# The last four slabs of each stage by token row, and the pieces behind them in column halves, in a two-block kernel

## The chip, the cores and the metric

One core of a Trainium2 chip runs the whole program. The metric is device microseconds of that core, the median of three runs. Lower is better.

## The reference, cut to what matters

Two transformer blocks in float32, one behind the other, on 256 tokens of width 2048. Each block is a mixer and a feed-forward part, and both have the same frame:

```python
h = rms_norm(x, g_pre_ffn) * (1.0 + scale_f) + shift_f      # second block: rmsnorm(h, g)
f = (silu(h @ w_ffn_gate) * (h @ w_ffn_up)) @ w_ffn_down
x = x + gate_f * rms_norm(f, g_post_ffn)                    # second block: h + rmsnorm(f, g)
```

So every stage ends in a row sum over 2048 columns (the post norm), an addition into x, and a second row sum (the next pre norm), before the next matrix can begin. The second block puts 16 meta tokens ahead of the 256 (272 columns), and its feed-forward part has a causal convolution over three tokens behind the gate product.

## The kernel before, in words

**Precision.** Each float32 matrix product is made of three passes in fp32r: high part by high part, high by low, low by high. A weight unit of 128x2048 floats (1 MB) lands in one of the four buffers of `raw` (RING = 4). ScalarE copies each half (1024 columns) to `whi` (`split_hi`, L446), VectorE writes the rest to `wlo` (`split_lo`, L453). Both have four slots (SLOTS = 4), and a slot is free when TensorE has counted `used` for what was in it. `raw_done` counts finished splits; SyncE's loads and TensorE both wait on it.

**Two kinds of product.** In a `chunk` (L557) the weight is the stationary side and x transposed (`xh`, `xl`) the moving one: eight halves of 24 matmuls. In a `slab` (L579) the staged activations (`stg`, cast by GpSimd in `stage_tile`, L618) are stationary and the weight moves: per half and per token row (t = 0 or 1, 128 tokens each) six matmuls into two PSUM banks (`products`, L568), so 24 for a slab. Row 0 has banks 0 to 3, row 1 banks 4 to 7.

**A feed-forward part** (`pe_ffn`, L1060) has two groups of 6 and 5 chunk pairs (gate, up), each followed by its 24 or 20 slabs of w_down. The first slab of a group does row 0, and waits for `h_done` ahead of row 1, since banks 4 to 7 hold the up product until VectorE has taken it (L1691). In the second group of the first block the sum `gateF` is taken out of banks 0 to 3 (`gate_out`) ahead of all slabs. The last two slabs (`last_slabs`, L602) do row 0 of both, count `rows_done`, then row 1 of both. VectorE adds a group's banks into `accf` (`parts`, L1712).

**Between stages.** For a row: VectorE multiplies by the gain (`dve_gained`, L1651), ScalarE sums the squares of 2048 columns (L648), VectorE adds into x (`dve_post`, L1658), ScalarE sums the squares of x, VectorE scales the row (`dve_normed_row`, L673), TensorE turns it 128 columns at a time (L690), ScalarE takes each turned tile to `xf` (L739), and VectorE splits `xf` in groups of four tiles (`dve_split_x`, L748 and L749); a chunk waits once per two halves for such a group. Eight tiles are turned ahead of the chunk, four more behind its second half and four behind its fourth (`pe_turn_more`). `pe_idle` (L698) issues small matmuls in the pause. Stage 2 (into the second block) also normalizes and turns the 16 meta rows, `xms`, behind row 1's. GpSimd fetches them when all slabs are staged (L2054) and multiplies `gateF` by the gain `gpost2` (L2058).

The four stage ends: A, out-projection of block one (sum 4, then norm 1); B, end of the first feed-forward part (sum 5, then norm 2); C, out-projection of block two (sum 6, then norm 3); D, the end of the program (sum 7, then the store of x).

## Time and profile before

| | |
|---|---|
| median of three runs | 2427.38 us (2423.9 to 2430.56) |
| profiled execution, its own time | 2429.2 us |
| its span | 2427.4 us |
| TensorE busy with matmuls | 2313.0 us (95%) |
| VectorE, ScalarE, GpSimd busy | 1530.9, 1047.7, 127.9 us |
| DMA | 506.47 MB, mean 209 GB/s |

The chain that ended last is the shortest explanation of the span: each piece of it released the next. Busy time of another engine counts only where it stands in that chain.

### The profile page before, as it was taken

Reading aid. Unit: us, or ns where it says so; the run is one execution under the profiler, and the core shown is the slowest. Engines: PE = TensorE matmul, PEld = TensorE weight load, DVE = VectorE, ACT = ScalarE, POOL = GpSimd, SP = SyncE. Lnnn points to the kernel's source line nnn. Section 1 sums busy time; section 2 is a strip of 40 time slices with the busy share of each in tenths; the row PEclk is TensorE's granted clock in tenths of the full one; section 3 lists DMA queues with packets and bytes.
Section 4 is the critical chain, followed back from the end, with each engine's and each line's share of the span. In section 5 each row is a group of like instructions: output and inputs, shape, how many; then the busy total and the mean of one; then the engine's idle time right before and its main releaser. Section 6 shows DMA issues by size and latency. Waiting matters only on the chain.

```text
span 2427.4 us, 41656 instructions
## 1 busy us (share of the span) xinstructions
PE 2313.0 (95%) x16346; PEld 2159.0 (89%) x16346; DVE 1530.9 (63%) x1727; ACT 1047.7 (43%) x1227; POOL 127.9 (5%) x248
## 2 busy tenths in 40 slices
PE   3999989899999999999999999998999999999997
PEld 3899768899998899998799998798999978999986
DVE  7988689755544467654554898746566544556545
ACT  5463243534444334443443535645444433344343
POOL 0000014000001100001100000000000011000010
PEclk9999989999999999999999999899999999999999
DMA  9988849555555577864455553254555555555552
GB/s 397 421 333 312 347 159 383 187 190 190 182 184 189 194 257 283 283 202 166 158 161 178 165 174 121 71 174 140 191 182 181 190 176 192 188 189 174 191 189 104
DMA packets 162957, 506.47 MB, mean 209 GB/s; under 512 B 8096, under 2 KB 12496, under 8 KB 134048
## 3 DMA queue, kind: packets, MB, share of 16 engines
q1 hardware_dynamic: 161536, 500.28, 58.8%
q0 software_dynamic: 752, 3.48, 0.5%
q8 instruction: 63, 1.03, 0.2%
q10 hardware_dynamic: 576, 1.44, 0.2%
q14 instruction: 30, 0.25, 0.0%
HBM read 503.07 MB, written 2.10 MB: 208 GB/s over the span
## 4 chain that ended last, share of the span: by engine, by line
PE 87%; DVE 5%; DMA 5%; ACT 2%; issue 1%; SPq 0%; POOL 0%; ACTq 0%; DVEq 0%; POOLq 0%
PE pb L574 23%; PE pb L552 18%; PE pb L554 18%; PE pb L553 18%; DMA raw<-w_in 3%; PE pb L536 1%; PE pb L932 1%; PE pb L537 1%; PE pb L538 1%; DVE x L1658 1%; PE pb L690 1%; DMA raw<-w_ada 1%; DVE wlo L499 1%; DVE raw L464 0%; DVE wlo L453 0%
## 5 line engine op out<-in xcount | busy, mean ns | idle before, releaser
L453 DVE TENSOR_TENSOR wlo<-raw,whi 128x1024 fp32r<-128x1024 f32 (+1 forms) x712 | 863.7, 1222 | 746.2 <-ACT whi L446 744.6
L446 ACT ACTIVATE whi<-raw 128x1024 fp32r<-128x1024 f32 (+1 forms) x712 | 746.3, 1054 | 1083.7 <-PE pb L554 715.4
L552 PE MATMUL pb<-xh,whi 128*128 128x256 f32 (+2 forms) x3760 | 1063.0, 283 | 5.8 <-DVE xl L749 3.0
L553 PE MATMUL pb<-xl,whi 128*128 128x256 f32 (+2 forms) x3760 | 1062.5, 283 | 0.0
L554 PE MATMUL pb<-xh,wlo 128*128 128x256 f32 (+2 forms) x3760 | 1061.4, 282 | 0.0
L552 PEld LDWEIGHTS pb<-xh,whi 128*128 128x128 f32 x3760 | 710.0, 189 | 6.8 <-ACT xf L739 4.0
L553 PEld LDWEIGHTS pb<-xl,whi 128*128 128x128 f32 x3760 | 709.9, 189 | 0.0
L554 PEld LDWEIGHTS pb<-xh,wlo 128*128 128x128 f32 x3760 | 709.6, 189 | 0.0
L574 PE MATMUL pb<-whi,stg 128*128 128x512 f32 x1664 | 453.0, 393 | 15.5 <-DVE hb L1691 5.1
L574 PEld LDWEIGHTS pb<-whi,stg 128*128 128x128 f32 x1664 | 315.1, 190 | 85.5 <-issue 6.8
L574 PE MATMUL pb<-wlo,stg 128*128 128x512 f32 x832 | 258.5, 392 | 0.0
L574 PEld LDWEIGHTS pb<-wlo,stg 128*128 128x128 f32 x832 | 158.1, 190 | 33.2
L464 DVE CUSTOM_DVE_ANT_0 raw<-raw,gateF,bcol 128x2048 f32<-128x2048 f32 x47 | 112.0, 2393 | 11.9 <-DMA raw<-w_ada 8.1
L622 POOL CAST stg<-hTh 128x256 fp32r x88 | 35.4, 402 | 1443.4 <-PE pb L554 1052.0
L508 PE MATMUL pb<-xh,whi 128*128 128x256 f32 (+1 forms) x256 | 73.6, 288 | 14.8 <-DVE wlo L499 7.9
L2467 DVE SCALAR_TENSOR_TENSOR zT<-upad,colv,zT x180 | 75.7, 481 | 0.0
L536 PE MATMUL pb<-xh,whi 128*128 128x256 f32 x240 | 69.1, 288 | 4.3 <-DVE wlo L453 4.3
L509 PE MATMUL pb<-xl,whi 128*128 128x256 f32 (+1 forms) x256 | 72.9, 285 | 0.0
L510 PE MATMUL pb<-xh,wlo 128*128 128x256 f32 (+1 forms) x256 | 72.8, 284 | 0.0
L690 PE MATMUL pb<-kc,xs 128*128 128x128 f32 x128 | 25.3, 355 | 45.3 <-ACT xs L2195 31.8
L537 PE MATMUL pb<-xl,whi 128*128 128x256 f32 x240 | 68.5, 285 | 0.0
L538 PE MATMUL pb<-xh,wlo 128*128 128x256 f32 x240 | 68.3, 285 | 0.0
(372 smaller groups left out, 1601.1 us busy)
## 6 DMA issues: line engine op xcount, KB each, us to landing
raw<-w_ada SPq DMA_DIRECT2D x79, 1024.0 KB, 7.0
raw<-w_ffn_gate SPq DMA_DIRECT2D x44, 1024.0 KB, 5.2
raw<-w_ffn_up SPq DMA_DIRECT2D x44, 1024.0 KB, 5.2
raw<-w_ffn_down SPq DMA_DIRECT2D x44, 1024.0 KB, 4.8
raw<-w_gate SPq DMA_DIRECT2D x44, 1024.0 KB, 5.2
raw<-w_up SPq DMA_DIRECT2D x44, 1024.0 KB, 5.2
raw<-w_down SPq DMA_DIRECT2D x44, 1024.0 KB, 4.8
raw<-w_in SPq DMA_DIRECT2D x40, 1024.0 KB, 5.1
```

What stands on the lines that cost most here:

```text
L446: act.activation(to, src, ACT.Copy).then_inc(hi_ready, 1)
L453: dve.tensor_tensor(to, src, hi, ALU.subtract).then_inc(raw_done, 1)
L464: return dve.tensor_tensor_reduce(unit, unit, csb[:, :], g, b, ALU.mult, ALU.add, to)
L508: mm(o, whi[:, s, wt], xh[:, k, 0:SEQ], start=(k == 0 and n % 2 == 0), stop=False, skip_group_check=True)
L536: mm(o, whi[:, s, t], xh[:, k, 0:SEQ], start=(k == 0 and f % 2 == 0), stop=False, skip_group_check=True)
L537: mm(o, whi[:, s, t], xl[:, k, 0:SEQ], start=False, stop=False, skip_group_check=True)
L538: last = mm(o, wlo[:, s, t], xh[:, k, 0:SEQ], start=False, stop=(k == KT - 1), skip_group_check=True)
L552: mm(o, whi[:, s, t], xh[:, k, c0:c1], start=(k == 0), stop=False)
L553: mm(o, whi[:, s, t], xl[:, k, c0:c1], start=False, stop=False)
L554: last = mm(o, wlo[:, s, t], xh[:, k, c0:c1], start=False, stop=(k == KT - 1))
L574: last = mm(pb[:, 4 * t + 2 * hh + c, :], stg[:, s, part, t * P:(t + 1) * P], wt[:, ws, c * CW:(c + 1) * CW], start=first and part == 0 an ...
L2467: op = dve.scalar_tensor_tensor(acc, src, wt, acc, ALU.mult, ALU.add)
```

## The change

- `last_slabs_by_row`: at the end of each feed-forward part row 0 of the last four slabs is done first (two slabs before), then row 1's first column half of all four, then its second half; `rows_done` is counted after each of the first two. So that four slabs can be held, the last two go through further buffers (`whix`, `wlox`, `stgx`) over `xh`, `xl` and `tb`. At A the same is done with two slabs; C is not a slab stage.
- `first_slabs`: the first two slabs of a group do one row of both, then the other row of both. In the second group of block one row 1 comes first.
- Sums and norms of row 1 in column halves (`act_half_stats`, `dve_post_halves`, `dve_normed_row`, `parts` with one half, the store in three pieces). VectorE's order changes: `dve_post` of row 0 now stands behind row 1's first half (FFN: ahead of it), and at A behind both halves of row 1's gain.
- Turned tiles lie two to a bank (`turn_at`), x is split in pairs of tiles and a chunk waits once per half.
- The meta rows are scaled by ScalarE in place and turned in a bank of their own ahead of the rest (`pe_turn_meta`), and VectorE writes them to `xf`; `turn` no longer has meta instructions.

The core of the diff:

```diff
+    whix = nc.alloc_sbuf_tensor_at("whix", [P, SLOTS, HALF], F32R, offset=XH0)
...
+        at_least(act, used, w - SLOTS - skipped + 1 + i * nw)
...
+    def far_hi(u, w, h):
+        act.wait_ge(landed[u % RING], landed_at(u, 0, 0))
+        act.activation(whix[:, h, :], raw[:, u % RING, h % 2 * HALF:(h % 2 + 1) * HALF], ACT.Copy).then_inc(hi_ready, 1)
+    def far_lo(u, w, h):
+        dve.wait_ge(hi_ready, w + 1)
+        dve.tensor_tensor(wlox[:, h, :], raw[:, u % RING, h % 2 * HALF:(h % 2 + 1) * HALF], whix[:, h, :].bitcast(F32),
+                          ALU.subtract).then_inc(raw_done, 1)
...
+            if x_split is not None:
+                pe.wait_ge(sem("x_split"), x_split + h + 1)
...
+        ws = 2 * s + hh if far else (w + hh) % SLOTS
+        tile, hi, lo = (stgx, whix, wlox) if far else (stg, whi, wlo)
+        for part, wt in ((0, hi), (0, lo), (1, hi)):
...
+    def first_slabs(u, w, stg_n, order, freed):
+        for n, t in enumerate(order):
+            if t in freed:
+                pe.wait_ge(*freed[t])
+            for j in range(2):
+                if n == 0:
+                    pe.wait_ge(staged, stg_n + 2 * j)
+                for hh in range(2):
+                    if n == 0:
+                        pe.wait_ge(raw_done, 2 * (u + j) + hh + 1)
+                    last = products(w + 2 * j, j, t, hh, j == 0)
+                if n:
+                    last.then_inc(used, 2)
...
+    def last_slabs_by_row(u, w, stg_n, n, step):
+        def one(j, t, hh):
+            return products(w + 2 * j, j % 2, t, hh, far=j >= 2)
+        for j in range(n):
+            pe.wait_ge(staged, stg_n + 2 * j)
+            for hh in range(2):
+                pe.wait_ge(raw_done, 2 * (u + step * j) + hh + 1)
+                last = one(j, 0, hh)
+        last.then_inc(sem("rows_done"), 1)
+        for hh in range(2):
+            for j in range(n):
+                last = one(j, 1, hh)
+                if hh:
+                    last.then_inc(used, 2)
+            if hh == 0:
+                last.then_inc(sem("rows_done"), 1)
...
+    def act_half_stats(n, hh, src, ready):
+        act.wait_ge(*ready)
+        part, total = stat[:, n, PART_AT:PART_AT + 1], stat[:, n, 1:2]
+        act_link(act.activation(like(squares[:, 0:HALF], src), src, ACT.Square, accum_out=total if hh else part))
+        if hh:
+            act.activation(total, total, ACT.Sqrt, scale=1.0 / D, bias=part).then_inc(sem("rms"), 1)
+        else:
+            act_link(act.activation(part, part, ACT.Identity, scale=1.0 / D, bias=eps))
...
+    def act_x_stats(n, t, done):
+        if t == 0:
+            act_row_stats(n, [(0, x[:, 0, :])], lambda t: (sem(done), 1))
+            return
+        for hh in range(2):
+            act_half_stats(n, hh, x[:, 1, COLS[hh]], (sem(done), 2 + hh))
...
-        dve.tensor_scalar(to, src, rstd[0:r, n, t:t + 1], None, ALU.mult).then_inc(sem("normed"), 1)
-    def turn_bank(n, k):
+        for cs in COLS if t else (slice(0, D),):
+            dve.tensor_scalar(to[:, cs], src[:, cs], rstd[0:r, n, t:t + 1], None, ALU.mult).then_inc(sem("normed"), 1)
...
-        return [rows[1], rows[0], rows[2]] if n == 2 else rows
+            return k % 8, 0
+        return 4 + k // 2 % 4, k % 2 * SEQ
...
+        pe.wait_ge(sem("normed"), NORMED_AT[2])
+        for k in range(KT):
+            last = pt(pb[:, META_BANK, k * META:(k + 1) * META], xm0[:, k * P:(k + 1) * P], kc[0:META, K_ID:K_ID + META])
+        last.then_inc(sem("turned"), 1)
...
-            pe.wait_ge(sem("turned_out"), KT * n + 1)
-            pe_idle(6, 4)
-            pe.wait_ge(sem("turned_out"), KT * n + 8)
+            pe_idle(3, 0)
...
+        def more(k0, k1, ready):
             pe.wait_ge(sem("turned_out"), KT * n + ready)
-            rows = turn_rows_of(n)
-            for k in range(k0, k0 + 4):
+            pe.wait_ge(sem("normed"), NORMED_AT[n] + 3)
...
+        return {1: lambda: more(8, 12, 4), 3: lambda: more(12, 16, 8)}
...
-            act.wait_ge(sem("turned"), KT * n + k + 1)
+            if n and k >= 8 and k % 2 == 0:
+                between(k // 2)
+            act.wait_ge(sem("turned"), TURNED_AT[n] + (k | 1 if n else k) + 1)
...
-        for j, hs in enumerate(((0, 1), (2, 3), (4,), (5, 6, 7))):
-            first(hs)
-            dve.wait_ge(ready, before + 4 * j + 4)
-            ks = slice(4 * j, 4 * j + 4)
+        first((0,))
+        for h in range(8):
+            dve.wait_ge(ready, before + 2 * h + 2)
+            ks = slice(2 * h, 2 * h + 2)
             dve_link(dve.tensor_copy(xh[:, ks, lo:width], xf[:, ks, lo:width]))
             dve.tensor_tensor(xl[:, ks, lo:width], xf[:, ks, lo:width], xh[:, ks, lo:width].bitcast(F32),
                               ALU.subtract).then_inc(sem("x_split"), 1)
+            if h < 7:
+                first((h + 1,))
...
+            order, freed = (0, 1), {1: (sem("h_done"), c + n)}
...
+                order, freed[0] = (1, 0), (sem("gate_out"), 1)
...
+            first_slabs(u, w, st + 2, order, freed)
+            for j in (2, 3):
+                slab(u + j, w + 2 * j, st + 2 * (j + 1), j % 2, False)
...
+            if g:
+                last_slabs_by_row(u + m, w + 2 * m, st + 2 * (m + 1), 4, 1)
+            else:
...
+            if g:
+                for h in range(4):
+                    far_hi(u - 2 + h // 2, w - 4 + h, h)
...
+            act_half_stats(n, hh, accf[:, 1, COLS[hh]], (sem("part_done"), summed + hh + 1))
...
+        if not hh:
+            dve_row_scale(n, t, P)
+        cs = slice(0, D) if hh is None else COLS[hh]
         dve.wait_ge(*taken)
-        dve.scalar_tensor_tensor(res, scaled, rstd[0:r, n, t:t + 1], res, ALU.mult, ALU.add).then_inc(sem(f"post{n}"), 1)
-        dve.wait_ge(sem(f"post{n}"), done)
-    def dve_ffn(b, u, w, gained):
+        dve.scalar_tensor_tensor(x[:, t, cs], xs[:, t, cs], rstd[:, n, t:t + 1], x[:, t, cs], ALU.mult, ALU.add)\
+           .then_inc(sem(f"post{n}"), 1)
+        dve.wait_ge(sem(f"post{n}"), t + 1 + (hh or 0))
+    def dve_post_halves(n, taken):
+        for hh in range(2):
+            dve_post(n, 1, taken, hh)
...
+                for h in range(4):
+                    far_lo(u - 2 + h // 2, w - 4 + h, h)
...
+                parts(0, (sem("rows_done"), ROWS[b, 0]))
                 first_lo(u, w, hs=(0, 1))
+                parts(1, (used, w))
+                first_lo(u, w, hs=(2, 3))
             else:
-                gained(0)
-            parts(1, (used, w))
-            if g + 1 < len(GROUPS):
-                first_lo(u, w, hs=(2, 3))
+                rows_end(parts, w)
...
+        for n, (t, cs) in enumerate(((0, slice(0, D)), (1, COLS[0]), (1, COLS[1]))):
+            sp.wait_ge(sem("post7"), n + 1)
+            sp.dma_start(out[0, t * P:(t + 1) * P, cs], x[:, t, cs]).then_inc(sem("stored"), 16)
+        sp.wait_ge(sem("stored"), 16 * 3)
...
+                    pool.wait_ge(sem("ht_ready"), c + n)
+                    for j in range(4):
+                        k = slice(4 * (n - 1) + j, 4 * n - 3 + j)
+                        far = j >= 2
+                        stage_tile(j % 2, hTh[:, k, :], hTl[:, k, :], 0 if far else w + 2 * (j - 1) + 8 * (n - 1),
+                                   to=stgx if far else stg)
...
+        last_slabs_by_row(U_WOUT + 28, W_WOUT + 28, 30, 2, 2)
...
-        pe_idle(22, 0)
+        pe_turn_meta()
+        pe_idle(18, 0)
...
+        act_row_stats(4, [(0, pb[:, 0:4, :])], lambda t: (sem("o_taken"), POST_AT[4] + 1))
+        act_half_stats(4, 0, pb[:, 4:6, :], (sem("o_taken"), POST_AT[4] + 2))
+        first_hi(U_FFN, W_FFN, hs=(0, 1))
+        act_half_stats(4, 1, pb[:, 6:8, :], (sem("o_taken"), POST_AT[4] + 3))
+        for t in range(NT):
+            act_x_stats(1, t, "post4")
...
+            act_row_stats(2, [(META_AT, xm0[:, :])], lambda t: (sem("meta_in"), 16), "meta_rms")
+            act.wait_ge(sem("x_rstd"), NT + 1)
+            act.activation(xm0[:, :], xm0[:, :], ACT.Copy, scale=rstd[0:META, 2, META_AT:META_AT + 1]).then_inc(sem("normed"), 1)
             act_post_ffn(5, 0)
-            first_hi(U_WIN2X, W_WIN2X, n=6 * P)
+            first_hi(U_WIN2X, W_WIN2X, n=6 * P, hs=(0,), skipped=SLOTS)
+            act_x_stats(2, 0, "post5")
+            act_post_ffn(5, 1, 0)
+            first_hi(U_WIN2X, W_WIN2X, n=6 * P, hs=(1,), skipped=SLOTS)
+            act_post_ffn(5, 1, 1)
+            act_x_stats(2, 1, "post5")
+            first_hi(U_WIN2X, W_WIN2X, n=6 * P, hs=(2, 3), skipped=SLOTS)
...
+        for t in range(NT):
+            act_x_stats(3, t, "post6")
...
+        for hh in range(2):
+            act_post_ffn(7, 1, hh)
...
-        for t in range(NT):
-            dve.wait_ge(*((sem("rms"), RMS_AT[4] + 2) if t else (sem("rows_done"), 1)))
-            dve_gained(4, pb[:, 4 * t:4 * t + 4, :], by_bank(adaA[:, :]), by_bank(xs[:, t, :]))
-            dve_post(4, t, xs[:, t, :], x[:, t, :], (sem("o_taken"), POST_AT[4] + t + 1), t + 1)
+        for ready, banks, t, cs in (((sem("rows_done"), ROWS[4]), slice(0, 4), 0, slice(0, D)),
+                                    ((sem("rows_done"), ROWS[4] + 1), slice(4, 6), 1, COLS[0]),
+                                    ((used, W_FFN), slice(6, 8), 1, COLS[1])):
+            dve.wait_ge(*ready)
+            o = pb[:, banks, :]
+            dve_gained(4, o, like(adaA[:, cs], o), like(xs[:, t, cs], o))
+        dve_post(4, 0, (sem("o_taken"), POST_AT[4] + 1))
+        dve_post_halves(4, (sem("o_taken"), POST_AT[4] + 3))
...
+            dve_gained(n, accf[:, t, cs], gateF[:, cs], xs[:, t, cs])
...
+            def rows_end(parts, w):
+                parts(0, (sem("rows_done"), ROWS[n]))
+                gained(n, 0)
+                dve_post(n, 0, (sem("o_taken"), POST_AT[n] + 1))
+                parts(1, (sem("rows_done"), ROWS[n] + 1), (0,))
+                gained(n, 1, 0)
+                ahead()
+                parts(1, (used, w), (1,))
+                gained(n, 1, 1)
+                dve_post_halves(n, (sem("o_taken"), POST_AT[n] + 3))
...
+            dve.wait_ge(sem("meta_rms"), 1)
+            at = rstd[0:META, 2, META_AT:META_AT + 1]
+            dve.reciprocal(at, stat[0:META, 2, META_AT:META_AT + 1]).then_inc(sem("x_rstd"), 1)
...
+        dve_normed_row(2, 0)
+        dve_normed_row(2, 1)
+        dve.wait_ge(sem("turned"), TURNED_AT[2])
+        g = col("g_pre_mix_2", 0, KT).rearrange("p (k o) -> p k o", o=1).to_broadcast([P, KT, META])
+        dve_link(dve.tensor_tensor(xf[:, :, 0:META], pb[:, META_BANK, 0:KT * META].rearrange("p (k t) -> p k t", t=META), g,
+                                   ALU.mult))
+        dve_split_x(T2, sem("turned_out"), 2 * KT,
+                    lambda hs: first_lo(U_WIN2X, W_WIN2X, n=6 * P, hs=[h for h in hs if h]))
...
+        dve_post(6, 0, (sem("o_taken"), POST_AT[7]))
+        dve_post_halves(6, (sem("o_taken"), POST_AT[7]))
```

## Rows read from the trace of the kernel before

**Rows 1.** The chain that ended last: share of the span by engine.

```profile
PE 87%; DVE 5%; DMA 5%; ACT 2%; issue 1%; SPq 0%; POOL 0%; ACTq 0%; DVEq 0%; POOLq 0%
```

**Rows 2.** Waits of TensorE: who for whom, us in total, times, longest.

```profile
PE pb L574 <- DVE hb L1691: 5.1, 3, 2.1
...
PE pb L574 <- ACT gateF L1357: 3.0, 1, 3.0
```

**Rows 3.** Windows: length, busy of each engine (instructions), granted clock, DMA share, GB/s.

```profile
440.40:456.50 16.10, 8.46 (x58) 7.70 (x57) 14.10 (x13) 14.29 (x21) 0.00 (x0) 0.79 0.09 24
...
735.00:856.50 121.50, 121.50 (x538) 100.64 (x537) 54.92 (x46) 46.57 (x44) 16.43 (x44) 1.00 0.54 191
...
1204.30:1222.80 18.50, 11.55 (x81) 10.87 (x80) 17.53 (x18) 12.28 (x21) 0.00 (x0) 0.82 0.08 17
1222.80:1245.00 22.20, 22.20 (x168) 20.63 (x169) 14.36 (x15) 10.07 (x15) 4.30 (x8) 1.00 0.65 181
...
2413.50:2427.40 13.90, 0.00 (x0) 0.00 (x0) 9.49 (x7) 2.88 (x5) 0.00 (x0) 0.59 0.37 151
```

**Rows 4.** Windows at the lower clock; first and last timeline row behind one stall.

```profile
1095.00:1098.00 3.00, 3.00 (x9) 2.35 (x8) 0.00 (x0) 0.00 (x0) 0.00 (x0) 0.50 0.00 0
1214.30:1221.20 6.90, 5.59 (x29) 5.26 (x30) 6.18 (x8) 4.22 (x10) 0.00 (x0) 0.51 0.00 0
...
1944.87 1.22 PE L574 MATMUL pb<-whi,stg 128*128 128x512 f32 x2 [2.12 <-DVE hb L1691]
...
1948.39 0.62 PE L574 MATMUL pb<-wlo,stg 128*128 128x512 f32 x2
```

**Rows 5.** Timeline: two VectorE instructions of 512 columns.

```profile
1612.07 1.47 DVE L1651 TENSOR_TENSOR xs<-pb,gateF 128x512 f32<-128x512 f32 x2 [1.47 <-PE pb L2151]
```

**Rows 6.** Timeline of stage end A.

```profile
435.21 2.29 DVE L1651 TENSOR_TENSOR xs<-pb,adaA 128x2048 f32<-128x2048 f32 x1 [1.00 <-PE pb L574]
...
447.83 1.91 ACT L648 ACTIVATE xf<-x 128x2048 f32<-128x2048 f32 x1 [0.77 <-DVE x L1658]
...
452.31 3.75 ACT L739 ACTIVATE xf<-pb,mods 128x256 f32<-128x256 f32 x8 [0.26 <-PE pb L690]
...
454.27 0.69 DVE L748 CAST xh<-xf 128x1024 fp32r<-128x1024 f32 x1 [0.32 <-ACT xf L739]
455.00 1.22 DVE L749 TENSOR_TENSOR xl<-xf,xh 128x1024 fp32r<-128x1024 f32 x1
```

**Rows 7.** Timeline of stage end B; last, its turning piece in the chain.

```profile
1195.21 5.10 POOL L2058 TENSOR_TENSOR gateF<-gateF,gpost 128x2048 f32<-128x2048 f32 x1
...
1204.33 2.35 DVE L1721 TENSOR_TENSOR accf<-accf,pb 128x1024 f32<-128x1024 f32 x2 [0.69 <-PE pb L574]
...
1211.59 2.35 DVE L1658 SCALAR_TENSOR_TENSOR x<-xs,rstd,x 128x2048 f32<-128x2048 f32 x1
...
1215.61 4.80 PE pb L690 x24
```

**Rows 8.** DMA issues: times, KB each, median us from issue to landing.

```profile
out<-x SPq DMA_DIRECT2D x2, 1024.0 KB, 3.9
...
gpost<-g_post_ffn SPq DMA_DIRECT2D x1, 1024.0 KB, 6.7
...
xm<-meta_tokens POOLq DMA_DIRECT2D x1, 128.0 KB, 2.9
```

**Rows 9.** Timeline of GpSimd: a cast while VectorE works.

```profile
429.39 1.34 POOL L622 CAST stg<-xh 128x256 fp32r x1 [3.70 <-PE pb L574]
```

**Rows 10.** Timeline of stage end C.

```profile
1653.90 2.35 DVE L1658 SCALAR_TENSOR_TENSOR x<-xs,rstd,x 128x2048 f32<-128x2048 f32 x1
...
1664.79 0.36 PE L552 MATMUL pb<-xh,whi 128*128 128x258 f32 x1 [1.41 <-DVE xl L749]
```

**Rows 11.** Timeline of stage end D.

```profile
2412.51 1.28 ACT L649 ACT_TABLE_LOAD   x1
...
2420.78 2.35 DVE L1658 SCALAR_TENSOR_TENSOR x<-xs,rstd,x 128x2048 f32<-128x2048 f32 x1
```

More of the change, by code:

```diff
@@ L566, in chunk, with products, slab @@
                 behind[h]()
-    def products(w, s, t, hh, first=False):
-        ws = (w + hh) % SLOTS
-        for part, wt in ((0, whi), (0, wlo), (1, whi)):
+    def products(w, s, t, hh, first=False, far=False):
+        ws = 2 * s + hh if far else (w + hh) % SLOTS
+        tile, hi, lo = (stgx, whix, wlox) if far else (stg, whi, wlo)
+        for part, wt in ((0, hi), (0, lo), (1, hi)):
             for c in range(2):
-                last = mm(pb[:, 4 * t + 2 * hh + c, :], stg[:, s, part, t * P:(t + 1) * P],
-                          wt[:, ws, c * CW:(c + 1) * CW], start=first and part == 0 and wt is whi,
+                last = mm(pb[:, 4 * t + 2 * hh + c, :], tile[:, s, part, t * P:(t + 1) * P],
+                          wt[:, ws, c * CW:(c + 1) * CW], start=first and part == 0 and wt is hi,
                           stop=part == 1, skip_group_check=True)
         return last
-    def slab(u, w, stg_n, s, first, i=0, nu=0, nk=0, freed=None):
+    def first_slabs(u, w, stg_n, order, freed):
[11 more added lines that the diff above has]
+                    last.then_inc(used, 2)
+    def slab(u, w, stg_n, s, first, i=0, nu=0, nk=0):
         def split(hh):
@@ L585, in slab @@
         pe.wait_ge(staged, stg_n + i * nk)
-        if freed is not None:
-            for t in range(NT):
-                if t:
-                    pe.wait_ge(*freed)
-                for hh in range(2):
-                    if t == 0:
-                        split(hh)
-                    last = products(w, s, t, hh, first)
-            last.then_inc(used, 2)
-            return
         for hh in range(2):
@@ L1094, in pe_ffn @@
             u, w, c = u + 8 * n, w + 16 * n, c + n
-            for j in range(4):
-                slab(u + j, w + 2 * j, st + 2 * (j + 1), j % 2, j == 0, freed=None if j else (sem("h_done"), c))
+            first_slabs(u, w, st + 2, order, freed)
+            for j in (2, 3):
+                slab(u + j, w + 2 * j, st + 2 * (j + 1), j % 2, False)
             with pe.Fori(1, n - 1) as i:
@@ L2502, in _ @@
         meta_sums(0)
-        for t in range(NT):
-            dve_post(6, t, xs[:, t, :], x[:, t, :], (sem("o_taken"), POST_AT[7]), t + 1)
+        dve_post(6, 0, (sem("o_taken"), POST_AT[7]))
+        dve_post_halves(6, (sem("o_taken"), POST_AT[7]))
         meta_scale(0)
```

178 lines of the change are left out of this document (78 added, 100 removed).

## The prediction, made before the changed kernel ran

> **What bounds the kernel now.** Start with the chain that ended last: TensorE carries 87% of it [rows 1]. So only two things count: how fast TensorE works, and where it stands still. Its waits come next [rows 2]. Slabs wait for `h_done` three times (5.1 us) and once for `gate_out` (3.0). The windows then give each pause its length [rows 3]: 16.1 us at stage end A, 18.5 at B, 13.9 behind the last matmul at D. In these TensorE's busy digits are turns and `pe_idle`, not useful products. The same view prices its work: 538 matmuls of slabs in 121.5 us is 0.226 each, so six are 1.36 us, a row of a slab (12) 2.72, a slab 5.44. In the first chunk behind B 168 instructions take 22.2 us; two blocks of 12 turns took 2.1 each, so the 144 products took 18.0: 0.125 each, 2.25 for a half of 18.
>
> Below, T is the end of the last product of a stage.
>
> **Group starts (`first_slabs`).** Before, TensorE has one slab-row (2.72 us) to do before it needs the banks that `h_done` frees; now two (5.44). The longest of the three stalls is 2.12 us [rows 4], so 2.72 more covers them all: 5.1 us gone. In the second group of block one, row 1 goes first and needs only `h_done`, which ends 0.1 us behind the ada rows; row 0's banks are read by ScalarE beneath 5.44 us of work, for a stall of 3.0: 2.9 gone. What is late next: both slots of slab 0 are given back at 8.2 us instead of one by one, and slab 2 is wanted at 10.9; ScalarE's copy, VectorE's rest and the staging have 2.7 us between them, and the second half is wanted 2.7 later still. Sum 8.0 us.
>
> Two of these four stalls cost more than their length. Behind the 2.12 us stall eight products begin within 3.52 us, at 1.22 and 1.05 us a pair, where the full clock needs 1.81; a window in the like place behind `gate_out` shows a granted clock of 0.50, which is 1.2 GHz [rows 4]. Each costs 1.7 us. Without the stall TensorE is busy before and after, so both go: 3.4 us.
>
> **Price of cutting.** Two VectorE instructions of 512 columns take 1.47 us [rows 5], one of 1024 takes 1.22 [rows 6]: a cut costs about 0.25. So a 2048 piece of 2.29 becomes 2.44. From the 1024 forms (0.69 and 1.22) a pair of tiles is 0.4 + 0.72 on VectorE. ScalarE's 2048 squares hold it 2.0 us (2.3 with the root); a half I take as 1.15 plus 0.3 for the small step; half of 2.0 and all of it are the bounds. The Trainium skill speaks against small pieces here: VectorE: DVE Perf Modes, The TRN2 errata, has every SBUF-source instruction pay a fixed extra latency and advises tiles of at least 512 elements. The trace agrees in the 0.25 us above.
>
> **A.** Row 0's gain starts 5.4 us ahead of T = 440.6 [rows 6], as now. Row 1's first half is ready at T-2.7, its second taken by T+1.25. Row 0's `dve_post` now stands behind that: T+1.45 to T+3.85, 2 us later than before. Row 1's halves end at T+6.5 (before T+7.2). But ScalarE is then the limit: x row 0 until T+6.2, two halves until T+9.1 (before T+9.5). The first half of the normed row at T+9.95, while ScalarE splits two weights until T+11.1; two turned tiles (eight take 3.75 [rows 6]) T+12.05; pair split and wake T+13.4. Before: T+15.9. Gain 2.5.
>
> **B.** The far buffers let splits run ahead: copies need no slot and end near T-16.5, rests near T-14.7. TensorE starts the third slab's row 0 at T-16.3 and the fourth's at T-13.6 (T less 8 slab-rows of 2.72, plus two and three); the splits are there 1.9 us or more before, the staging 1.6. Row 0 is ready at T-10.9, but two things hold VectorE. (a) `gateF` times `gpost2`, 5.1 us on GpSimd [rows 7], needs a load that takes 6.7 us [rows 8], issued by SyncE at about T-18.9, behind the load that waits for the second of these slabs: it lands at T-12.2, gate ready at T-7.1. (b) VectorE waits for the meta root ahead of row 0's sums. A GpSimd cast is under 0.4 us with VectorE mostly at rest (16.43 us for 44 in [rows 3]) and 1.34 with it busy [rows 9]; here the far rests run through the last staging, so I take 1.34, and the meta load starts at T-15.3, lands T-12.4 (2.9 for its 128 KB [rows 8]), and squares, table load and root end at T-8.7. The Trainium skill has the reason: in the GPSIMD Engine Reference, Specifications, both share SBUF interfaces, in contention when VectorE has two SBUF inputs. With the short casts everything here is 0.8 us earlier.
>
> From T-8.6: sums of row 0 (2.35), gain (2.29), post (0.2 + 2.35) to T-1.3; row 1 first half, sum and gain, to T+1.2; a weight rest (0.95) and the second half to T+4.6; root T+4.9; post halves to T+7.5, where before it was T+9.65 [rows 7]. ScalarE ends x's halves at T+9.25; first half normed T+10.1; turns; two tiles T+11.65 to 12.3; first matmul near T+13.3, by clock. Before T+18.5: 5.2. It is so much because 24 turns (4.80 us at the lower clock, [rows 7]) become 8 behind the last row, and the meta row no longer stands between. In the chunk two blocks of 12 turns at 2.1 become 8 at 0.87: 2.5. B: 7.7. The 16 meta turns and 18 idle matmuls fill T to T+6.3, hidden by the pause.
>
> VectorE per half of the chunk: pair 0.42 + 0.75, rest 0.95, gaps 0.1: 2.2 against TensorE's 2.25. That is tight; at A and C it is 2.45 against 2.85.
>
> **C.** There are no slabs. Row 1's post is in halves that end 0.1 us later, x's sum 0.2 later (the second half is behind ScalarE's row 0). The split can begin with two tiles of four: two tiles at 0.4 and half of 1.9 saved, and row 1 turned from half a row (0.65 sooner), less the 0.2 and less the 0.6 in which TensorE still turns row 0. From 1653.90 (row 1's post) to 1664.79 (first matmul) [rows 10], 10.9 us, I get 1.6 less; bounds 0.8 (the tiles alone) and 2.4.
>
> **D.** The last product ends T = 2413.5. Row 0's sums start at T-10.9; its root waits for squares and the 1.28 us table load [rows 11] until T-4.8; post to T-2.25; row 1's first half to T+0.2; second to T+2.6; root T+2.9; halves stored at T+4.3 and T+5.5. Before, the last post ended at 2423.13, T+9.6. The store lands 3.9 us after issue [rows 8]; for half the bytes I take 3.5, bounds 2.9 (the 128 KB load) and 3.9. End T+9.4 against T+13.9: 4.5.
>
> **Sum.** 8.0 + 3.4 + 2.5 + 7.7 + 1.6 + 4.5 = 27.7 us. The profiled execution took 2429.2 (span 2427.4), 1.8 above the median of the runs shown: 2401.5 for it, 2399.7 for the median. I say 2400.
>
> Unchanged: DMA bytes, products, the first chunk of the program. At A the DMA share was near full ahead of T, so T itself stays. The loads behind B start earlier by up to 3 us, behind the gain load on SyncE.
>
> **Rivals.**
> 1. *The stage ends give little* (0.09). ScalarE, already the limit at A, or the late gate at B takes the place of the waits removed; only group starts and D count: 8.0 + 3.4 + 4.5 = 15.9, 2411. For it: at A ScalarE's end moves only 0.4. Against: turning by halves and pairs saves time behind ScalarE, too.
> 2. *Low clock at the new starts* (0.15). In the pauses the clock fell to 0.51 over 6.9 us [rows 4] and was back before the chunk. Starting 1.6 to 5 us earlier, up to three chunks could begin at 1.2 GHz; at a loss like the 1.7 us behind the group starts each: 5.1, 2405. The Trainium skill (TensorE: Matmul & The Clock Gate, Part 1) says that how many matmuls begin at the lower clock varies from run to run; one profile cannot show it.
> 3. *VectorE becomes the bound in the chunks split by pairs* (0.03), the one that ends slower. 21 handovers, seven in each of three chunks. For each 0.1 us a handover exceeds TensorE's half, 2.1 us are lost. To eat 27.7 it must exceed it by 1.32, that is a cycle of 3.6 us at B, 4.2 at A and C; at 4.7 us everywhere it would be 2443. Against: it is summed from rows as 2.2 to 2.45.
> 4. *It doesn't do what it says* (0.03). The far splits come late, TensorE waits in the last slabs, and rows 0 and 1 end together; group starts alone, 11.4, are kept, and in each of two stages up to two slab-rows (5.4 in all of a possible 10.9) are lost again: 2421.4. Against: the slack of 1.6 us above.
>
> The forecast has 0.70, its own range 2396 to 2404. The range: below, D's store at 2.9 (0.6), GpSimd at 0.40 (0.8), and C at 2.4 (0.8) make 2397.8, and some three more for what the sum may have missed where it took the longer value (ScalarE's halves): 2394; above, rivals 1 and 2 to 2410. A change of 0.3% (7.3 us) is what a measurement of this kernel can tell: faster 0.94, within 0.03, slower 0.03.
>
> **What would show it.** No wait of slabs on `hb` or `gateF`, clock 1.00 behind group starts; first chunk matmul 13.4 us behind the last product at A, about 13.3 at B; turns x8 in the chunk behind B; end 9.4 us behind the last product. Wrong, if row 0's L1721 starts later than T-8 at B or D, if a chunk's L552 waits for L749 after its first half, or if last slabs show a gap.

## The result and the profile after

The changed kernel takes 2403.07 us (median of 6 runs, 2398.32 to 2406.47), the kernel before 2428.19 beside it (6 runs, 2423.9 to 2431.55): a ratio of 0.9895, 95% interval 0.9878 to 0.9912, 25.1 us less. The forecast was 2400, in a range of 2394 to 2410. The profiled execution took 2398.32, its span is 2396.5 against 2427.4.

The waits of TensorE come first again, in the same columns (total, times, longest). Of [rows 2], `hb` has one wait of 0.2 us left, and `gateF` has none. The turns at A and B wait for the normed rows as they did before. First the row of the kernel before, then two of the changed one:

```profile
PE pb L690 <- DVE xs L673: 12.5, 3, 6.4
```

```profile
PE pb L743 <- DVE xs L728: 10.8, 2, 5.4
...
PE pb L588 <- DVE hb L1774: 0.2, 1, 0.2
```

That is no new wait: three of 12.5 us in all have become two of 10.8, one at A and one at B. The windows give the pauses their lengths now: A, three microseconds behind a group start in block one, B, and the part of B at the lower clock.

```profile
435.80:449.00 13.20, 7.44 (x50) 7.07 (x49) 11.74 (x15) 12.92 (x25) 0.00 (x0) 0.74 0.02 7
1082.00:1085.00 3.00, 2.84 (x13) 2.36 (x13) 1.35 (x2) 2.83 (x2) 0.00 (x0) 1.00 0.92 319
1191.30:1206.60 15.30, 9.66 (x75) 9.28 (x74) 13.08 (x18) 12.43 (x24) 0.00 (x0) 0.78 0.01 1
1198.90:1205.30 6.40, 3.25 (x16) 3.29 (x17) 4.80 (x8) 5.21 (x11) 0.00 (x0) 0.50 0.00 0
```

A lasts 13.2 us, B 15.3, where they were 16.1 and 18.5 [rows 3]; behind the group start the clock is 1.00 and 13 matmuls begin, where it was 0.50 and 9 [rows 4]. B improved less than the forecast says: it has the chunk start 13.3 us behind the last product. The timeline of B shows where: VectorE stands for 6.97 us until ScalarE has the root of the meta row, and only then are row 0's sums taken.

```profile
1171.01 1.39 POOL L664 CAST stgx<-hTh 128x256 fp32r<-128x256 f32 x1
1172.36 1.39 POOL L665 CAST stgx<-hTl 128x256 fp32r<-128x256 f32 x1
...
1180.42 1.91 ACT L690 ACTIVATE xf<-xm 16x2048 f32<-16x2048 f32 x1 [5.96 <-DMA xm<-meta_tokens]
...
1184.06 0.15 DVE L2560 RECIPROCAL rstd<-stat 16x1 f32<-16x1 f32 x1 [6.97 <-ACT stat L691]
1184.14 2.35 DVE L1809 TENSOR_TENSOR accf<-accf,pb 128x1024 f32<-128x1024 f32 x2
...
1197.78 2.61 DVE L1736 SCALAR_TENSOR_TENSOR x<-xs,rstd,x 128x1024 f32<-128x1024 f32 x2
...
1206.65 0.39 PE L565 MATMUL pb<-xh,whi 128*128 128x272 f32 x1 [0.28 <-DVE xl L810]
```

With the last product at 1191.3, the sums start 7.2 us ahead of it and the chunk 15.3 behind. At A the ordering is as forecast: ScalarE's two weight copies, then the turned tiles, then the chunk 13.3 us behind the last product (435.8).

```profile
444.68 1.99 ACT L448 ACTIVATE whi<-raw 128x1024 fp32r<-128x1024 f32 x2
446.71 3.30 ACT L800 ACTIVATE xf<-pb,mods 128x256 f32<-128x256 f32 x7
...
449.02 0.35 PE L565 MATMUL pb<-xh,whi 128*128 128x256 f32 x1 [0.42 <-issue]
```

At D the last product ends at 2387.6, the span 8.9 us later. Row 1's last halves end at 2393.5 and the rest is the store; the DMA issues have each half of row 1 at 2.6 us, not the 3.5 that I took.

```profile
2376.77 2.35 DVE L1809 TENSOR_TENSOR accf<-accf,pb 128x1024 f32<-128x1024 f32 x2 [3.40 <-PE pb L588]
...
2390.87 2.61 DVE L1736 SCALAR_TENSOR_TENSOR x<-xs,rstd,x 128x1024 f32<-128x1024 f32 x2
```

```profile
out<-x SPq DMA_DIRECT2D x1, 1024.0 KB, 3.9
out<-x SPq DMA_DIRECT2D x2, 512.0 KB, 2.6
```

### The profile page after: what moved, and what is told of

Read it like the earlier page. It is cut to its first block, busy times and chain, and to the rows that moved or that the text cites. A ratio compares the mean times of both kernels' runs of the same rounds, so it can differ in the third digit from the quotient of the medians.

```text
span 2396.5 us, 41646 instructions
## 1 busy us (share of the span) xinstructions
PE 2299.6 (96%) x16320; PEld 2150.4 (90%) x16320; DVE 1533.6 (64%) x1761; ACT 1050.8 (44%) x1246; POOL 123.3 (5%) x248
## 4 chain that ended last, share of the span: by engine, by line
PE 87%; DVE 5%; DMA 4%; ACT 2%; issue 1%; POOL 0%; DVEq 0%; ACTq 0%; POOLq 0%; SPq 0%
PE pb L588 22%; PE pb L565 19%; PE pb L566 19%; PE pb L567 19%; DMA raw<-w_in 3%; PE pb L549 1%; PE pb L551 1%; PE pb L550 1%; PE pb L995 1%; PE pb L743 1%; DVE x L1736 1%; DMA sigc<-w_ada 1%; DVE wlo L512 1%; ACT xf L690 0%; DVE raw L477 0%
## 5 line engine op out<-in xcount | busy, mean ns | idle before, releaser
L455 DVE TENSOR_TENSOR wlo<-raw,whi 128x1024 fp32r<-128x1024 f32 (+1 forms) x704 | 854.0, 1222 | 714.1 <-ACT whi L448 712.6
L448 ACT ACTIVATE whi<-raw 128x1024 fp32r<-128x1024 f32 (+1 forms) x704 | 737.4, 1054 | 1043.3 <-PE pb L567 702.2
L588 PE MATMUL pb<-whi,stg 128*128 128x512 f32 x1600 | 433.0, 391 | 7.2 <-DVE wlo L455 5.4
L588 PEld LDWEIGHTS pb<-whi,stg 128*128 128x128 f32 x1600 | 301.3, 189 | 73.8 <-issue 7.1
L588 PE MATMUL pb<-wlo,stg 128*128 128x512 f32 x800 | 247.9, 391 | 0.0
L588 PEld LDWEIGHTS pb<-wlo,stg 128*128 128x128 f32 x800 | 151.3, 189 | 31.7
L664 POOL CAST stg<-hTh 128x256 fp32r (+1 forms) x84 | 35.8, 427 | 1407.2 <-PE pb L567 1048.7
L521 PE MATMUL pb<-xh,whi 128*128 128x256 f32 (+1 forms) x256 | 73.2, 286 | 15.3 <-DVE wlo L512 8.7
```

The source lines that it names most:

```text
L448: act.activation(to, src, ACT.Copy).then_inc(hi_ready, 1)
L455: dve.tensor_tensor(to, src, hi, ALU.subtract).then_inc(raw_done, 1)
L521: mm(o, whi[:, s, wt], xh[:, k, 0:SEQ], start=(k == 0 and n % 2 == 0), stop=False, skip_group_check=True)
L588: last = mm(pb[:, 4 * t + 2 * hh + c, :], tile[:, s, part, t * P:(t + 1) * P], wt[:, ws, c * CW:(c + 1) * CW], start=first and part == 0 a ...
```

## The experiments

All start from the changed kernel and were timed or profiled beside the kernel before. The runs of one of these kernels lie 4 to 15 us apart, so most effects are read from the stretches of a profile. In the table, worked out from TensorE's timeline of each, "out" is the end of the first out-projection; A, B and D run from the last product of a stage to the first product of the next chunk (D: to the end of the span); C runs from the last chunk of the second out-projection to the next one; the other columns are the work between. The forecast's 10.9 us at C began at row 1's post.

```
kernel            ratio (95%)            out    A     A-B    B     B-C    C     C-D    D
before            1                     440.6  15.9  747.8  18.5  424.7  17.3  748.7  13.9
before_again      -                     436.8  15.9  746.2  18.5  430.9  17.3  748.8  13.9
changed           0.9895 (.9878-.9912)  435.8  13.3  742.3  15.3  421.9  16.1  743.0   8.9
again             0.9888 (.9871-.9906)  434.5  13.5  742.3  15.4  421.9  16.1  743.0   8.9
starts_undone     0.9942 (.9926-.9957)  436.6  13.4  747.8  15.7  426.6  16.1  751.0   8.9
fours             0.9928 (.9907-.9948)  439.8  15.2  743.8  17.1  422.4  18.1  742.4   8.9
meta_early        0.9874 (.9855-.9893)  436.4  13.5  742.9  12.3  426.7  16.1  743.0   8.9
meta_gate_early   0.9875 (.9853-.9897)  438.4  13.3  742.4  11.3  426.8  16.1  743.1   8.9
more_idle         0.9894 (.9870-.9918)  438.6  14.7  742.3  17.6  426.3  17.1  742.4   8.9
idle_to_fit       0.9875 (.9857-.9893)  437.5  13.3  742.3  14.7  426.2  15.2  742.4   8.9
best              0.9871 (.9853-.9889)  438.7  13.3  742.3  11.0  427.7  15.2  742.4   8.9
two_slabs_d       -                     434.2  13.3  742.3  15.5  426.2  16.1  742.8  14.4
whole_d           0.9898 (.9881-.9916)  437.4  13.3  742.4  15.4  422.1  16.1  743.0  11.7
cast_twice        -                     441.1  13.7  742.6  16.0  426.6  16.6  742.6   8.9
```

**What of the difference is chance.** Two runs have no edit: the changed kernel again, and the kernel before again.

> The changed kernel once more, as the measure for the runs beside it, and for how much of the 30.9 us between the two profiled spans is the change. Forecast: about 25 us less than the kernel before. In the profile the last product of the first out-projection ended 4.85 us earlier than before, at 435.75 against 440.6, though no edit stands ahead of it but the order of the last two slabs. If that is chance, this run ends it anywhere from 434 to 442, and the stretches behind it keep their lengths (13.3 us at A, 15.3 at B, 8.9 at D) within 0.3. If it is the change, it ends near 435.8 again.

> The kernel before once more, for what of its stretches is chance. The last product of the first out-projection ended at 434.2 to 441.1 in eight profiles of changed kernels, so the 440.6 of before is not the change's: here anywhere in 434 to 442. The stretch between the chunk at B and the out-projection's last chunk took 424.7 before and 421.9 after, but 426.2 to 426.8 in six other kernels, with the clock at 0.50 for longer among the short waits of the second mixer. If that is chance, it may take 424.7 or about 429.3 here; A 15.9, B 18.5, D 13.9 and the stretches between stay.

"out" lies between 434.2 and 441.1 in all fourteen profiles, at 440.6 and 436.8 for the one kernel before. So 4.85 us of the 30.9 between the two profiled spans are chance, and 26.05 are left, near the 25.1 between the medians. How near is partly luck: counted against the second profile of the kernel before, the same difference is 30.7. B to C has two levels, 421.9 to 422.4 and 426.2 to 427.7 for changed kernels; the kernel before shows both itself, 424.7 and 430.9. The windows of the second mixer tell them apart; here 90 us of the kernel before and of the same kernel again:

```profile
1470.00:1560.00 90.00, 85.02 (x520) 66.82 (x519) 69.28 (x213) 58.22 (x147) 3.08 (x3) 0.92 0.16 55
```

```profile
1470.00:1560.00 90.00, 84.90 (x486) 64.74 (x485) 64.73 (x202) 56.83 (x144) 3.08 (x3) 0.87 0.15 47
```

Granted clock 0.92 against 0.87, and 34 matmuls fewer in the same time. TensorE waits 0.5 to 1.2 us a few times there, and the clock falls for longer or shorter behind these waits. Behind one and the same wait of 1.0 us (for `zT`, L1833) it stayed at 1.00 in the first profile and was 0.50 in the second, here for the 10 us from 1.8 us behind the wait's end:

```profile
1508.40:1518.40 10.00, 9.30 (x49) 5.76 (x49) 3.90 (x22) 7.02 (x21) 0.00 (x0) 1.00 0.00 0
```

```profile
1504.80:1514.80 10.00, 10.00 (x27) 5.49 (x27) 1.92 (x11) 4.62 (x10) 0.00 (x0) 0.50 0.00 0
```

Which level a run is in was nobody's edit; the first profile of the kernel before and that of the changed kernel, on which the steps below are measured, were both on the shorter one. The Trainium skill (TensorE: Matmul & The Clock Gate, Part 1), as the forecast cites it, has the number of matmuls at the lower clock vary between runs; the two traces agree, with 6.1 us between them.

**Group starts back as they were.**

```diff
-            first_slabs(u, w, st + 2, order, freed)
-            for j in (2, 3):
+            if 0 in freed:
+                pe.wait_ge(*freed[0])
+            pe.wait_ge(staged, st + 2)
+            for t in range(NT):
+                if t:
+                    pe.wait_ge(*freed[1])
+                ...
+                    last = products(w, 0, t, hh, True)
+            last.then_inc(used, 2)
+            for j in (1, 2, 3):
```

> The changed kernel with the first slab of each group taken alone again, as before. If the group starts carry what the sum has for them, 11.4 us are lost against the changed kernel run beside it: 5.1 of h_done and 3.0 of gate_out as waits, and 1.7 twice for the lower clock behind two of them. If only the waits count, 8.0. If the low clock in the pauses was there anyway, the windows behind the starts show 0.50 in both. The rival that stage ends give little says that this is nearly all of the change: 11.4 of it, with the end D 4.5.

Ratio 0.9942 against 0.9888: 13 us slower. By stretches 5.5 and 8.0, 13.5. The waits are back, and the lower clock is behind three of the four starts (windows of 4 us, clock third from the end):

```profile
PE pb L588 <- DVE hb L1784: 5.1, 3, 2.1
...
PE pb L588 <- ACT gateF L1435: 3.0, 1, 3.0
```

```profile
1086.00:1090.00 4.00, 2.87 (x7) 2.30 (x8) 0.57 (x1) 1.08 (x1) 0.00 (x0) 0.68 0.34 143
1938.00:1942.00 4.00, 4.00 (x14) 3.13 (x13) 1.14 (x1) 0.52 (x1) 0.38 (x2) 0.65 0.17 70
2298.00:2302.00 4.00, 2.87 (x7) 2.29 (x8) 2.31 (x2) 1.06 (x1) 0.00 (x0) 0.65 0.64 246
```

Waits 8.1 and 1.7 three times: 13.2. Before, it was two of four, and in the kernel before again one: its A to B is 1.6 us shorter, since behind the same wait of 3.0 us for `gateF` the clock stayed at 1.00 there, where [rows 4] has 0.50.

```profile
1091.20:1094.20 3.00, 3.00 (x14) 2.46 (x14) 0.00 (x0) 0.00 (x0) 0.00 (x0) 1.00 0.00 0
```

So the forecast's 3.4 us is a draw of a term that ran from 1.7 to 5.1. What the change gained there in the two profiles is 5.5 + 5.7 = 11.2 us, forecast 11.4.

**x in fours again.**

```diff
-        first((0,))
-        for h in range(8):
-            dve.wait_ge(ready, before + 2 * h + 2)
-            ks = slice(2 * h, 2 * h + 2)
+        first((0, 1))
+        for j in range(4):
+            dve.wait_ge(ready, before + 4 * j + 4)
+            ks = slice(4 * j, 4 * j + 4)
```

> The changed kernel with x split in fours of tiles again and not in pairs; turns and everything else stay. The first chunk at A, B and C then waits for four tiles: two tiles at 0.47 on ScalarE, and 0.27 and 0.50 on VectorE more (0.69 and 1.22 against 0.43 and 0.73), 1.7 us at each, so 5.1 us slower if pairs gain what the steps say. The rival that VectorE becomes the bound by pairs says the opposite: fewer instructions on it, no loss, or a gain. If ScalarE's four tiles are hidden at one place, 3.4.

A 1.9, B 1.7, C 2.0 longer: 5.6, near the 5.1. The stretches behind A and B lose 1.5 and 0.5 more. The 1.5 are the clock: TensorE waits for nothing more behind the start of the chunk, but the clock falls in it, and 29 matmuls stand in 5 us where the changed kernel has 42 at 1.00 (449.0 to 454.0).

```profile
455.00:460.00 5.00, 4.98 (x29) 5.00 (x30) 4.02 (x4) 0.50 (x1) 0.00 (x0) 0.66 0.77 255
```

Where the 0.5 lie is open. The chunk behind C wins 0.6, since it now begins at the full clock. In all some 7 us by the stretches (by the ratios, 0.9928 and 0.9888, nearer 10, with intervals of 4 to 5 us either way), won by an edit that adds 12 pairs of VectorE instructions.

**Is VectorE near its limit in the chunks?** The cast of each pair is made twice.

```diff
-            dve_link(dve.tensor_copy(xh[:, ks, lo:width], xf[:, ks, lo:width]))
+            for _ in range(2):
+                dve_link(dve.tensor_copy(xh[:, ks, lo:width], xf[:, ks, lo:width]))
```

> The changed kernel with VectorE's cast of each pair of tiles of x made twice in the chunks at A, B and C: 0.45 us more for each of 24 pairs. The handover then takes 2.65 us by the 2.20 of A and 2.4 by the 1.98 of B. TensorE's half of a chunk takes 2.9 us at A and C and 2.2 at B. If VectorE has the room that the steps say, only the first pair counts at A and C (0.45 each) and at B 0.45 and up to 0.2 for each of seven: 1.4 to 2.8 us in all. If VectorE already sets the pace in these chunks, 24 times 0.45: 10.8.

0.4 us at A, 0.7 at B, 0.5 at C and 0.3 behind A: some 1.9 us, not 10.8 (behind C it is 0.4 less). B to C is on the longer level, with seven other profiles of changed kernels; the chunk behind B itself takes 20.1 us there and 19.9 in the changed kernel. A cycle of cast, rest and weight rest takes 2.19 us at A in the changed kernel (2.45 forecast) and 1.98 at B (2.2), since the instructions overlap by 0.1; the two rows of `xl` stand 2.19 apart:

```profile
448.23 0.69 DVE L810 TENSOR_TENSOR xl<-xf,xh 128x512 fp32r<-128x512 f32 x1
...
450.42 0.69 DVE L810 TENSOR_TENSOR xl<-xf,xh 128x512 fp32r<-128x512 f32 x1
```

The rival that VectorE becomes the bound had its point 1.3 us beyond TensorE's half; the chunks stand on the other side of it, with 0.3 us of room at B and more at A and C.

**The meta load early, then the gain load too.** First only the first hunk; then both. The old issue of each load goes.

```diff
+                if g and b == 0:
+                    pool.wait_ge(staged, 2 * KT + 2 * (4 * sum(GROUPS) - 4))
+                    pool.dma_start(xm0[:, :], a["meta_tokens_2"]).then_inc(sem("meta_in"), 16)
                 if g:
                     pool.wait_ge(sem("ht_ready"), c + n)
                     for j in range(4):
...
+                        if j == 2 and b == 0:
+                            pool.wait_ge(staged, 2 * KT + 2 * (4 * sum(GROUPS) - 2))
+                            pool.dma_start(gpost2[:, :], row("g_post_ffn", 0, D).to_broadcast([P, D]))\
+                                .then_inc(sem("gpost2_in"), 16)
```

> The changed kernel with the load of the meta rows issued four slabs earlier, before the last four are staged. At B VectorE waited 6.97 us for their root, to T-7.3, with row 0's sums behind that wait. With the rows there early the sums start when row 0 is done, T-10.9, and end at T-8.5; then the product of the gates, ready at T-6.0, is the next to be late, where row 0's gain began at T-4.8. Forecast: 1.2 us less at stage end B and in the time. If it is the gates alone that hold row 0 there, nothing; if nothing else is late, 3.5.

B takes 12.25 us, 3.1 less, where I had expected 1.2. The first VectorE row is the sums, now waiting for TensorE alone; the second, the gain, waits for the gates:

```profile
1181.91 2.35 DVE L1809 TENSOR_TENSOR accf<-accf,pb 128x1024 f32<-128x1024 f32 x2 [2.34 <-PE pb L588]
1185.64 2.29 DVE L1727 TENSOR_TENSOR xs<-accf,gateF 128x2048 f32<-128x2048 f32 x1 [1.37 <-POOL gateF L2152]
```

The last product ends at 1192.75, so the sums start 10.8 us ahead of it and the gates are ready 7.1 ahead, not 6.0. The DMA issues around B say why the gates came sooner as well. First the changed kernel, then this run:

```profile
gpost<-g_post_ffn SPq DMA_DIRECT2D x1, 1024.0 KB, 8.1
xm<-meta_tokens POOLq DMA_DIRECT2D x1, 128.0 KB, 6.4
```

```profile
gpost<-g_post_ffn SPq DMA_DIRECT2D x1, 1024.0 KB, 6.8
xm<-meta_tokens POOLq DMA_DIRECT2D x1, 128.0 KB, 3.0
```

With the two issued 1.4 us apart, as in the changed kernel, the gain load took 8.1 to 8.4 us and the meta load 6.4 to 6.7 in all nine profiles that have both in these places. The gain load's own issue did not move here (18.7 us ahead of the last product in both), so its 1.3 us are the meta load's doing. With the other load out of the way they take about the 6.7 and 2.9 us of [rows 8], on which the forecast stood. The mean busy share of the DMA engines, second from the end, tells the two places of the meta load apart, while it is in flight, first in the changed kernel, then here:

```profile
1174.10:1180.40 6.30, 6.30 (x29) 5.21 (x29) 2.99 (x3) 0.35 (x1) 0.42 (x1) 1.00 1.01 329
```

```profile
1161.40:1164.40 3.00, 3.00 (x15) 2.49 (x14) 1.51 (x2) 1.06 (x1) 0.42 (x1) 1.00 0.44 96
```

> As the run with the early meta load, and the gain load too is issued early: by GpSimd, between the staging of the second and the third of the last four slabs at B, not by SyncE two microseconds later behind a weight load. In the run with the early meta load alone the gates' product ended 7.1 us ahead of the last product, row 0's sums 8.5 ahead of it, and stage end B took 12.25 us. If the gates are what is late next, row 0's gain starts up to 1.4 us earlier, its post then waits for the root of ScalarE, and the rows of the second half wait for their own products: 0.5 to 1.4 us less, B 10.9 to 11.8. If the gain load lands late again beside the weight loads, or GpSimd's cast of the next slabs waits for its own DMA instructions, B stays at 12.3 or TensorE stands in the last slabs.

B 11.26 us, 1.0 less again: the gain now starts 8.4 us ahead of the last product, right behind the sums. From GpSimd the load lands in 4.6 us:

```profile
gpost<-g_post_ffn POOLq DMA_DIRECT2D x1, 1024.0 KB, 4.6
xm<-meta_tokens POOLq DMA_DIRECT2D x1, 128.0 KB, 3.1
```

The casts behind it were slow (three of them 1.39 to 1.40), and the gates' product began behind them, 1.0 us behind the landing; nothing on TensorE or VectorE waited for either. The rival for the 6.4 us is VectorE, whose last far rests ran beside the meta load in the changed kernel. Against it: here all four ran from 1174.6 to 1180.0, beside the gain load, and it was the fastest of the three. So I put the 6.4 us down to the other traffic, the gain load and the weight loads around it. That is argued from these runs and not shown by one that changes nothing else; nor is it shown why the gain load is faster from GpSimd. The Trainium skill (SBUF — State Buffer, SBUF: two separate sides) warns that a load issued by GpSimd can stand still for want of descriptors while VectorE runs an instruction in a 2-port perf mode, as a float32 copy within SBUF does. The far rests are differences of two tensors (TENSOR_TENSOR) and no such copies, so no run here shows it.

**Keeping the clock up in the pauses.**

```diff
-        pe_idle(14, 0)      # A
+        pe_idle(50, 0)      # then 32
-        pe_idle(18, 0)      # B
+        pe_idle(58, 0)      # then 36
-        pe_idle(14, 3)      # C
+        pe_idle(48, 3)      # then 30
```

> The changed kernel with 36, 40 and 34 more idle matmuls at A, B and C, 0.118 us each, in pauses of 5.4, 5.4 and 4.4 us in which TensorE stands still. The granted clock fell to 0.50 in each pause and the 16 turns behind took 3.65 us. If the clock stays at 1.00, the turns take about 1.9; at B the first tiles come 0.9 us earlier, at C too, where six or so products of the chunk ran at half the rate (0.7 more), and at A nothing, since ScalarE's two weight copies end there at the same time as the turns: about 2.5 us less in all. If the low clock costs nothing where it lies, 0. If the clock falls all the same, the idle matmuls take 0.215 us each and delay the turns by up to 3 us each.

A miss of arithmetic: a call comes out as two matmuls, which I had not counted. At A 100 of them take 11.33 us and end well behind the rows, so A, B and C are 1.4, 2.2 and 1.0 us longer; but the 16 turns behind take 1.91 us, at 1.00.

```profile
438.48 11.33 PE L751 MATMUL pb<-kc 128*128 128x128 f32 x100
449.64 1.91 PE L743 MATMUL pb<-kc,xs 128*128 128x128 f32 x16
```

> The changed kernel with idle calls that end inside the pauses. In the run with more idle calls each came out as two matmuls of 0.118 us, 0.235 a call, so that they reached 3 us and more past the rows; but the clock stayed at 1.00 and the 16 turns took 1.91 us where they took 3.65. Here 18, 18 and 16 calls more, 4.2, 4.2 and 3.8 us, in pauses of 5.4, 5.4 and 4.4. If the lower clock costs what stands behind it: B 0.9 less (14.4), C 1.3 to 1.6 less (14.6), A the same (13.3), since ScalarE's weight copies end there with the turns. About 2.4 in all. If nothing of it lies on the path, 0.

B 14.73 (0.6 less), C 15.15 (0.95 less), the work behind C 0.6 less, A unchanged: 2.2 us, forecast 2.4. The clock is 1.00 through all of B:

```profile
1193.10:1207.90 14.80, 12.22 (x112) 11.61 (x111) 13.45 (x18) 12.53 (x25) 0.00 (x0) 1.00 0.00 0
```

**D: slabs or halves?** The first kernel takes two slabs by row in the second block and drops the far buffers there; the second keeps four and takes row 1 whole.

```diff
-            if g:
-                last_slabs_by_row(u + m, w + 2 * m, st + 2 * (m + 1), 4, 1)
+            if g and b:
+                for j in (m, m + 1):
+                    slab(u + j, w + 2 * j, st + 2 * (j + 1), j % 2, False)
+                last_slabs_by_row(u + m + 2, w + 2 * m + 4, st + 2 * (m + 3), 2, 1)
```

```diff
+                if n == 7:
+                    parts(1, (used, w))
+                    ...
+                    dve_gained(n, accf[:, 1, :], gateF[:, :], xs[:, 1, :])
+                    dve_post(n, 1, (sem("o_taken"), POST_AT[n] + 2))
+                    return
```

> The changed kernel with the last two slabs and not the last four by token row in the second block, at D alone, with no far buffers there; the column halves stay. If the four slabs carry what the steps say, row 0 is whole 5.4 us ahead of the last product and not 10.9: its sums, gain, root with the 1.28 us table load and post then run into the work of row 1, and VectorE has 2.35 + 2.29 + 2.35 for row 0 and as much for row 1 from T-5.4 on, with 1.3 in waits for the root: the last post ends near T+10 and the store near T+12.9 against T+8.9, 4.0 us slower. The stretches elsewhere stay. If halves alone make the gain at D, it stays at 9.

> The changed kernel with row 1's sum, gain, norm, post and store in one piece at D, and the last four slabs by row as they are. In the run with two slabs only, and halves, D took 14.37 us, 0.5 more than before the change, so the halves alone give nothing there. With four slabs and no halves: row 1's banks are read from T on, 2.35, gain 2.29, squares and root 2.3 beside it, post 2.35 to T+7.3 by the gain's end and T+7.3 by the root, and a store of 1024 KB that takes 3.9: near T+11.4, so 2.5 slower than 8.9. If the slabs are all of it, D stays at 9; if the two are worth the same, 11.5; at 13.9 halves are what counts and slabs are only their condition.

14.4 and 11.7 us, against 8.9 with both and 13.9 with neither. With two slabs and halves D is 0.5 slower than before: VectorE has row 0 in hand until 3.2 us behind the last product, at 2390.3; by then both halves of row 1 are long whole. As I read the rows, nothing is then won by taking them apart, and there are more instructions to make:

```profile
2391.16 2.35 DVE L1740 SCALAR_TENSOR_TENSOR x<-xs,rstd,x 128x2048 f32<-128x2048 f32 x1
2393.55 1.22 DVE L1813 TENSOR_TENSOR accf<-accf,pb 128x1024 f32<-128x1024 f32 x1
```

The four slabs alone give 2.2 us, the halves on top 2.8. Neither part can be priced without the other.

**A version that has it all.** Both loads early, with 32, 25 and 30 idle calls.

> Meta load and gain load early, and idle calls to fit at A, B and C. In the run with both loads early B took 11.26 us. With the clock at 1.00 in its turns 0.5 to 0.9 less, 10.5; C 14.6; A 13.3. Against the changed kernel 4.9 us at B and 1.5 at C: 6.4 less if each keeps its own, some 31 us less than before. If idle matmuls and the shorter pause together only move a wait to ScalarE's copies, 4 to 5.

B 11.02, C 15.15, A 13.29: 4.3, 0.95 and 0.6 (behind C) us less than the changed kernel, 5.9 in these stretches. At B the idle calls give only 0.2 here. The time is 2400.28 us (4 runs, 2396.77 to 2401.33), ratio 0.9871, interval 0.9853 to 0.9889, against 0.9888 (0.9871 to 0.9906) and 0.9895 for the changed kernel. The intervals overlap: that it is faster shows in the stretches, and the timing does not settle it; in its profile B to C, where the edit changes nothing, was on the longer level.

## Why the prediction was right, step by step

| Step | Forecast | Two profiles | Shown by |
|---|---|---|---|
| Group starts, waits and clock | 11.4 | 11.2 | starts_undone |
| A | 2.5 | 2.6 | fours, in part |
| B, to the chunk | 5.2 | 3.1 | meta_early |
| B, turns in the chunk | 2.5 | 2.8 | the chunk alone: 2.5 |
| C | 1.6 | 1.2 | fours, idle_to_fit |
| D | 4.5 | 5.0 | two_slabs_d, whole_d |
| Sum | 27.7 | 26.05 | median: 25.1 |

- **Group starts.** Right, and for the reasons given. Of the 3.4 us for the clock the size is chance: one to three of four starts fall to the lower level. Against the second profile of the kernel before, with one, the gain is 9.7.
- **A.** Right to 0.1 us: ScalarE is the limit. The split by pairs gives 1.9 of it (fours). That the clock was low in the turns cost nothing there (idle_to_fit).
- **B** is the term that was mis-sized: 5.2 us, measured 3.1. The step that failed is (b), "the meta load starts at T-15.3, lands T-12.4 (2.9 for its 128 KB)". It started at T-17.3, 2 us earlier, since only the last two casts were slow, but it took 6.4, beside the gain load that step (a) puts in flight at the same time, and landed at T-10.9; the gain load took 8.1 and not 6.7. The sums began at T-7.2, later than the T-8 that the forecast named as the sign that it would be wrong there. Each price was read where the other of the two was not in flight. The last post ended at T+9.1, forecast T+7.5: that is 1.6 of the 2.0 us by which B is longer than forecast. The other 0.4 are behind it, where the turns ran at the lower clock; with the clock at 1.00 B was 0.6 shorter (idle_to_fit). With the meta load out of the way the gates were ready at T-7.1, the very number of step (a), and B took 12.25 us. The forecast's own order, without the meta row's 0.9 us (gain from T-7.1, not T-6.2), makes that 12.4.
- **The turns in that chunk**: 8 in 1.04 us, twice, for two blocks of 12 at 2.1. From its first product to the first of the next chunk is 19.9 us, where it was 22.4: 2.5, as forecast. The 2.8 of the table is all of B to C, a stretch that can differ by 6 us by chance; that both profiles have the shorter level is luck.
- **C.** Inside its bounds. The pairs give 2.0 (fours), more than the whole gain, so the rest of the change costs 0.7 there. The chunk began at the lower clock, 0.95 and 0.6 us of which idle matmuls get back.
- **Price of cutting.** The forecast took 0.25 us from instructions that read different memories (PSUM and SBUF); on one kind it holds: an addition into x of 2048 columns takes 2.35 us, in two halves 2.61.
- **D.** The store of the half took 2.6 us, under my lower bound of 2.9; the last halves ended at T+5.9, forecast 5.5.

Of the rivals, "the stage ends give little" is out: without D they gave 9.7 of 26 us. "Low clock at the new starts" held at C alone, and cost 0.6 us of the products behind it where 5.1 had been put on three starts. VectorE does not set the pace (cast_twice). The splits by row came in time: no wait in the last slabs.

## What to carry to other kernels

At D, cutting the work behind the last product paid only with the products reordered so that there was a half to work on; alone it lost 0.5 us, together they gave 5.0. The split of x by pairs needed no such order and gave 5.6 at three stage ends. A load that is moved to where another is issued has to be priced with that other one in flight, and both of them; here 6.7 and 2.9 us became 8.1 and 6.4. And before a difference of two profiles is explained, the stretches that no edit touches are compared first: here they held 5 us by themselves, and 6 more between two profiles of one kernel.
